# The first Strassen block of two feed-forward parts: load order and the order of VectorE, GpSimd and ScalarE

## The reference

```python
D_MODEL, SEQ, D_FF, FFN_RES, EPS = 1024, 1024, 2816, 0.5, 1e-6

def _rmsnorm(x, g):
    xf = x.astype(jnp.float32)
    y = xf * lax.rsqrt(jnp.mean(xf * xf, axis=-1, keepdims=True) + EPS)
    return (y * g.astype(jnp.float32)).astype(x.dtype)

def _swiglu(h, w_gu, w_down):
    g, u = jnp.split(h @ w_gu, 2, axis=-1)
    return (jax.nn.silu(g) * u) @ w_down

for l in range(DEPTH_2):          # DEPTH_2 = 1
    x = x + FFN_RES * _swiglu(_rmsnorm(x, norm_ffn1[l]), w_ffn1_gu[l], w_ffn1_down[l])
    ...
    x = x + FFN_RES * _swiglu(_rmsnorm(x, norm_ffn2[l]), w_ffn2_gu[l], w_ffn2_down[l])
```

## Time and profile before

| | before |
|---|---|
| runs | 3335.28, 3335.58, 3343.84 us; median 3335.58 |
| the profiled execution | 3338.5 us, with a span of 3336.4 us |
| mean granted clock of TensorE | 0.993 of full speed |
| TensorE busy | 3248.6 us (97% of the span), 19068 matmuls |
| VectorE busy | 1818.1 us (54%), 2813 instructions |
| GpSimd busy | 1803.1 us (54%), 1352 instructions |
| ScalarE busy | 1131.2 us (34%), 2104 instructions |
| first feed-forward part, plain pairs to the third block | about 1179 to 1265 us of the span |
| the same stretch of the second | 1550.87 us later |

### The profile page before, as it was taken

The page is one execution under the profiler, slowest core; times in us unless marked ns, Lnnn a source line. Parts: engine busy times, 40 slices in busy tenths (PEclk is TensorE's granted clock), DMA queues, the critical chain, the costliest instruction groups (busy, mean ns, idle before and its releaser), DMA issues.

```text
span 3336.4 us, 47997 instructions
## 1 busy us (share of the span) xinstructions
PE 3248.6 (97%) x19068; PEld 1655.5 (50%) x19068; DVE 1818.1 (54%) x2813; ACT 1131.2 (34%) x2104; POOL 1803.1 (54%) x1352
## 2 busy tenths in 40 slices
PE   8999998999999799999999999999999999999999
PEld 4555653655565344444445545555545444444444
DVE  4365558236545887775113376665666687676100
ACT  1434422233341523231002455555555342323000
POOL 4555752446675277674333465555665438777332
PEclk9999999999999999999999999999999999999999
DMA  3112112112021211112222111111112121111312
GB/s 133 41 49 62 59 61 90 53 40 77 26 89 39 82 56 58 64 51 98 71 67 93 32 53 53 56 48 52 36 53 90 47 101 53 62 64 38 109 52 79
DMA packets 59275, 211.70 MB, mean 63 GB/s; under 512 B 7344, under 2 KB 7728, under 8 KB 58544
## 3 DMA queue, kind: packets, MB, share of 16 engines
q1 hardware_dynamic: 54304, 191.34, 17.6%
q10 hardware_dynamic: 4752, 17.30, 1.3%
HBM read 181.36 MB, written 20.97 MB: 61 GB/s over the span
## 4 chain that ended last, share of the span: by engine, by line
PE 94%; DVE 3%; issue 1%; ACT 1%; POOL 1%; DMA 0%; DVEq 0%; POOLq 0%; ACTq 0%
PE pair L1184 27%; PE pair L1185 26%; PE pair L1186 26%; PE pair L1404 3%; PE pair L1373 3%; PE pair L1385 2%; PE pair L1622 1%; PE pair L1648 1%; PE pair L1633 1%; PE pair L1576 1%; PE pair L1204 1%; DVE arena L2155 1%; PE pair L1362 0%; POOL panel_parts L967 0%; ACT residual L1905 0%
## 5 line engine op out<-in xcount | busy, mean ns | idle before, releaser
L1184 PE MATMUL pair<-operand,panel_parts 128*128 128x512 f16 x1808 | 693.2, 383 | 47.8 <-DVE operand L2155 26.1
L966 POOL TENSOR_SCALAR panel_parts<-panel_raw 128x1024 f16<-128x1024 f32 (+3 forms) x204 | 209.0, 1024 | 920.7 <-issue 654.4
L1185 PE MATMUL pair<-operand,panel_parts 128*128 128x512 bf16 x1808 | 690.6, 382 | 0.0
L1186 PE MATMUL pair<-operand,panel_parts 128*128 128x512 f16 x1808 | 690.4, 382 | 0.0
L1184 PE MATMUL pair<-arena,panel_parts 128*128 128x512 f16 (+1 forms) x1248 | 471.3, 378 | 8.9 <-issue 4.4
L967 POOL TENSOR_TENSOR panel_parts<-panel_raw,panel_parts 128x1024 bf16<-128x1024 f32 (+3 forms) x204 | 469.2, 2300 | 17.0
L1003 POOL TENSOR_SCALAR arena<-arena,row_inv 128x256 f32<-128x256 f32 (+7 forms) x256 | 344.6, 1358 | 236.4 <-DVE row_inv L2221 236.1
L1185 PE MATMUL pair<-arena,panel_parts 128*128 128x512 bf16 (+1 forms) x1248 | 470.5, 377 | 0.0
L1186 PE MATMUL pair<-arena,panel_parts 128*128 128x512 f16 (+1 forms) x1248 | 470.3, 377 | 0.0
L1184 PEld LDWEIGHTS pair<-operand,panel_parts 128*128 128x128 f16 x1808 | 177.5, 98 | 283.1 <-issue 94.8
L2158 DVE SCALAR_TENSOR_TENSOR residual<-pair,residual 128x1024 f32<-128x1024 f32 (+1 forms) x64 | 61.3, 958 | 420.0 <-PE pair L1186 392.1
(11 more groups left out here) (300 smaller groups left out, 5979.1 us busy)
## 6 DMA issues: line engine op xcount, KB each, us to landing
panel_raw<-in_wl SPq DMA_DIRECT2D x58, 512.0 KB, 3.5
panel_raw<-in_wm SPq DMA_DIRECT2D x56, 512.0 KB, 3.6
ffn_extra<-in_wgu SPq DMA_DIRECT2D x18, 1024.0 KB, 5.0
panel_raw<-in_wgu SPq DMA_DIRECT2D x18, 1024.0 KB, 5.1
panel_raw<-in_wdn SPq DMA_DIRECT2D x32, 512.0 KB, 3.5
residual<-residual_spill SPq DMA_DIRECT2D x31, 512.0 KB, 6.9
residual_spill<-residual ACTq DMA_DIRECT2D x24, 512.0 KB, 2.6
panel_raw<-in_wgu SPq DMA_DIRECT2D x16, 512.0 KB, 3.6
```

Source lines behind the costliest of these rows:

```text
L966: chained(nc.gpsimd.tensor_scalar(hi[:, c], RAW[:, s, c], HI_MAX, -HI_MAX, ALU.min, ALU.max))
L1184: nc.tensor.matmul(out, stat[0], mov[0], start=first, stop=False, skip_group_check=skip)
L1185: nc.tensor.matmul(out, stat[0], mov[1], start=False, stop=False, skip_group_check=skip)
L1186: return nc.tensor.matmul(out, stat[1], mov[0], start=False, stop=last, skip_group_check=skip)
```

## The change

- `SQT`: the eight squares have their homes in 8192 columns of `arena`, none in `EXR`.
- SP: the raw weights of block 0 are loaded right behind the first turn's four panels, with no wait; the other blocks' loads are as they were.
- ScalarE: `weight_part(0, 0)` stands behind the first SiLU instead of the second; `term_part(B_T4)` stands before the weights 5 and 6 instead of behind them.
- GpSimd: `term_rest(B_T4)` stands behind `weight_rest(0, 4)` instead of `weight_rest(0, 6)`.
- VectorE: the four `weight_sum(0, n)` stand before `plain_pair(1)`; `plain_pair(3)` is cut into `plain_front(3)` and `plain_back(3)`, with `term_clip(B_T4)` and `evict(0, 0)` between them; `evict(0, 1)` and `evict(0, 2)` stand before the `weight_sum(1, n)`.

No arithmetic is added or left out. The diff:

```diff
--- before.py
+++ after.py
@@ -464,7 +464,7 @@
         GAINED, SQSUM, ROOT = [SIL[1], AF[1]], STAT[:, 0:T], STAT[:, T:2 * T]
         EX = sb("ffn_extra", [P, 4608])
         EXR = EX[:, 0:2048]
-        SQT = [arena(c, 1024) for c in (11264, 12288, 26624, 27648, 22528, 24576)] + [EXR[:, 0:1024], EXR[:, 1024:2048]]
+        SQT = [arena(8192 + 1024 * k, 1024) for k in range(KT)]
         SILP, AFP = [arena(2048 + 1024 * s, 1024) for s in range(2)], [arena(4096 + 1024 * s, 1024) for s in range(2)]
 
         XPF = XP.rearrange("p a c -> p (a c)")
@@ -865,21 +865,24 @@
                     layer_panel(l, name)
 
             def ffn(idx):
+                def raw(b):
+                    f = PLAIN_F + b
+                    dst = EXR.rearrange("p (j c) -> p j c", j=2) if b % 2 == 0 else RAW[:]
+                    src = io[f"wgu{idx}"][f // 2, 2 * (f % 2):2 * (f % 2) + 2].rearrange("j p c -> p j c")
+                    sp.dma_start(dst, src).then_inc(raw_loaded[b % 2], 16)
+
                 for i in range(PLAIN_F // 2):
                     for j in range(4):
                         panel(f"gu{idx}", i, j, io[f"wgu{idx}"][i, j])
-                for b in range(BLOCKS):
-                    f = PLAIN_F + b
-                    if b == 0:
-                        sp.wait_ge(square_added, 7 * idx)
-                    elif b == 1:
+                    if i == 0:
+                        raw(0)
+                for b in range(1, BLOCKS):
+                    if b == 1:
                         for j in (2, 3):
                             sp.wait_ge(panel_split[panel_slot(f"gu{idx}", j)], panels_before(f"gu{idx}", PLAIN_F // 2 - 1, j) + 2)
                     else:
                         sp.wait_ge(weight_lo, 7 * block_of(idx, b - 1))
-                    dst = EXR.rearrange("p (j c) -> p j c", j=2) if b % 2 == 0 else RAW[:]
-                    src = io[f"wgu{idx}"][f // 2, 2 * (f % 2):2 * (f % 2) + 2].rearrange("j p c -> p j c")
-                    sp.dma_start(dst, src).then_inc(raw_loaded[b % 2], 16)
+                    raw(b)
                 sp.wait_ge(weight_lo, 7 * BLOCKS * idx)
                 for i in range(2):
                     for j in range(12):
@@ -1073,9 +1076,11 @@
                     nc.gpsimd.tensor_tensor(lo, q, hi, ALU.subtract).then_inc(term_ready_pool, 1)
 
                 term_rest(B_T2, Q22, 0)
-                for i in range(7):
+                for i in range(5):
                     weight_rest(0, i)
                 term_rest(B_T4, Q21, 1)
+                for i in range(5, 7):
+                    weight_rest(0, i)
                 for b in range(1, BLOCKS):
                     for i in range(7):
                         weight_rest(b, i)
@@ -1959,17 +1964,18 @@
                     nc.scalar.activation(SILH[h], SILH[h], ACT.Silu).then_inc(half_silu, 1)
 
                 plain_silu(0)
+                weight_part(0, 0)
                 for home, q, n in ((B_T1, Q11, 9), (B_T3, Q12, 10), (B_T2, Q22, 11)):
                     term_part(home, q, n)
                 plain_silu(1)
-                for i in range(5):
+                for i in range(1, 5):
                     weight_part(0, i)
                 for f in range(2, PLAIN_F):
                     plain_silu(f)
+                act.wait_ge(tile_ready[3], tiles_before(f"gu{idx}", PLAIN_F // 2, 3))
+                term_part(B_T4, Q21, 12)
                 for i in range(5, 7):
                     weight_part(0, i)
-                act.wait_ge(tile_ready[3], tiles_before(f"gu{idx}", PLAIN_F // 2, 3))
-                term_part(B_T4, Q21, 12)
                 for b in range(BLOCKS):
                     first_copy(b)
                     if b + 1 < BLOCKS:
@@ -2566,12 +2572,19 @@
                 restart()
 
                 def plain_pair(f):
+                    plain_front(f)
+                    plain_back(f)
+
+                def plain_front(f):
                     i, j = divmod(f, 2)
                     g = ready(f"gu{idx}", i, 2 * j)
                     tt(AFP[j], g[:, :], ROOT, ALU.mult).then_inc(tile_taken[2 * j], 1)
                     u = ready(f"gu{idx}", i, 2 * j + 1)
                     dve.wait_ge(silu_made[j], i + (PLAIN_F // 2 * (idx - 1) + 1))
                     tt(AFP[j], u[:, :], SILP[j], ALU.mult).then_inc(tile_taken[2 * j + 1], 1)
+
+                def plain_back(f):
+                    i, j = divmod(f, 2)
                     dve.wait_ge(tile_taken[2 * j + 1], tiles_before(f"gu{idx}", i, 2 * j + 1) + 1)
                     chained(tt(AFP[j], AFP[j], ROOT, ALU.mult))
                     t = slice(f * T, (f + 1) * T)
@@ -2651,25 +2664,32 @@
                 term_sum(Q12, Q22, Q12, 10, 9)
                 term_sum(Q22, Q22, Q11, 11, 10)
                 term_sum(Q21, Q21, Q22, 12, 11)
-                plain_pair(1)
                 for n in range(4):
                     weight_sum(0, n)
+                plain_pair(1)
                 term_clip(B_T2, 3).then_inc(term_clipped, 1)
                 term_split(B_T1, Q11, 1)
                 plain_pair(2)
                 term_split(B_T3, Q12, 2)
-                plain_pair(3)
+                plain_front(3)
                 term_clip(B_T4, 4).then_inc(term_clipped, 1)
+                evict(0, 0)
+                plain_back(3)
                 for b in range(BLOCKS):
                     more = b + 1 < BLOCKS
                     if b > 0:
                         keep_block(b - 1)
-                    evict(b, 0)
+                    if b > 0:
+                        evict(b, 0)
+                    else:
+                        evict(b, 1)
+                        evict(b, 2)
                     if more:
                         for n in range(4):
                             weight_sum(b + 1, n)
-                    evict(b, 1)
-                    evict(b, 2)
+                    if b > 0:
+                        evict(b, 1)
+                        evict(b, 2)
                     for step in (3, 4, 5):
                         evict(b, step)
                 keep_block(BLOCKS - 1)
```

## The result

| | before | the change |
|---|---|---|
| median of the 19 runs of each | 3339.49 us (3335.28 to 3343.95) | 3345.63 us (3341.73 to 3349.92) |
| ratio, 95% interval | | 1.0015 (1.0009 to 1.0021) |
| the profiled execution, its span | 3338.5, 3336.4 us | 3341.73, 3339.6 us |

The change makes the kernel slower by 0.15% (5.0 us, 3.0 to 7.0, by the ratio; the two medians lie 6.1 us apart). That is less than the 0.3% which a few runs can tell from no change; it took 19 of each.

A forecast was written before the change was run, and what follows sets the result against it. TensorE bounds the kernel, with 13.0 us of its waits and low clock to win. Per feed-forward part 5.81 + 1.11 + 2.54 + 1.7 (clock) = 11.16 us; 22.3 for both, less 13.0, is +9.3 on 3335.6: 3344.9 us, range 3329 to 3350.

The forecast's parts named there:

- (a): VectorE's four weight sums, now before the second plain pair, meet GpSimd's panel split: 5.4 us, 2.8 more, done at 1194.4.
- (b): VectorE's second plain pair runs into the next panel's split, waits for its clip and subtraction, and ends at 1203.8.
- (c): VectorE's remainder waits for GpSimd's 2048-column remainder, issued first: ends at 1211.2 against 1205.03, 6.1 us late.
- (d): Third pair and remainder end at 1223.7; the fourth pair's second half starts at 1226.0 instead of 1219.73.
- (e): ScalarE's copies follow to 1229.2, the eviction ends at 1230.0: first block's fourth product 2.85 us late (0.68 before).
- (f): Pair's second half waits for GpSimd's moved remainder; first block's sixth product 5.81 us late in total, against 4.49.
- (g): Second block's sums lie between third and fourth eviction; the second block's fourth product comes 1.11 us later than possible.
- (h): Third block's sums wait for GpSimd's sixth weight of the second (1253.3); second block's sixth product 2.54 us late.
- rival A: VectorE keeps its place, fourth product on time, sixth 0.5 late, second-block waits stay: -1.4 us, 3334.2; chance 0.14 with D.
- B: The stall goes whole, second-block waits too, GpSimd's sixth weight done by 1246: -12.0 us, 3323.6; chance 0.13.
- C: As forecast, but the lag reaches the third block and each gap costs 2.7 of clock: 3350 us; chance 0.07.
- D: The change does nothing, TensorE's late products being held by GpSimd's weights alone: 3335.6 us; chance 0.14 with A.

The follow-up runs named there:

- Experiment 3: The changed kernel with GpSimd's 2048-column remainder for B_T2 issued as four instructions of 512 columns: ratio 1.0008 to before.
- 1: The changed kernel with the four weight sums of block 0 behind plain_pair(1) again: ratio 0.9993 to before.
- experiment 4: The changed kernel with evict(0, 1) and evict(0, 2) behind the second block's weight sums again: ratio 1.0033 to before.
- 6: The changed kernel with plain_pair(3) in one piece, B_T4's clip and evict(0, 0) behind it: ratio 1.0013 to before.
- 5: The changed kernel with GpSimd's remainder for B_T4 back behind the block's last weight: ratio 1.0020 to before.
- 7: The kernel before with only the squares' new homes and the early raw load of block 0: ratio 1.0006 to before.
- the first of 11: The kernel before with evict(b, 1) and evict(b, 2) ahead of the next block's weight sums in the first two blocks alone: ratio 0.9985.
- 2: The kernel before with the early raw load, its homes and the four weight sums ahead of plain_pair(1): ratio 1.0033 to before.
- 10: The kernel before with evict(0, 1) and evict(0, 2) ahead of the second block's weight sums, in the first block alone: ratio 0.9987.
- 8: The kernel before with evict(b, 1) and evict(b, 2) ahead of the next block's weight sums in every block: ratio 0.9951.
- second of 11: The kernel before with evict(b, 1) and evict(b, 2) ahead of the next block's weight sums from the third block on: ratio 0.9985.

## Why the prediction was right

It said slower, +9.3 us, by VectorE and GpSimd meeting at other places. Measured: 5.0 us (3.0 to 7.0) in the timed runs, 7.3 us in the two parts of the profile. So direction and mechanism held, and the size was put too high: 9.3 lies outside the interval. That the time itself came so near, 3344.9 foreseen and 3345.63 measured, is luck: the median of three runs that it was added to was 3.9 us below that of 19, which makes up for most of the excess.

- **(a), (b)** were right: sums of 1.52 and 2.50 us, all four done at 1190.2, that is 1194.3 in the times of before (1194.4 predicted), and a pair behind which the next instruction starts at 1199.64, that is 1203.7 (1203.8).
- **(c)** was right: a row of 6.04 us where VectorE's remainder was predicted to wait. Experiment 3 shows that it is the length of GpSimd's instruction, and 1 that it hangs on the sums' place.
- **(d), (e)**: the fourth pair's second row at 1225.9 in the times of before (1226.0); product 4 2.69 late (2.85).
- **(f)**: product 6 5.66 late (5.81). "About 4 us worse" without the moved evictions: 5.1 at product 6 itself, but only 2.0 and 3.2 in the lateness of a whole part (experiment 4), since the moved evictions bring waits to the second block. "About 1" for the split pair: 0.2 to 0.5 at product 6, nothing in the whole (6).
- **(g), (h)**: 1.04 (1.11) and 2.52 (2.54). The wait for GpSimd's sixth weight of the second block is there: it ends at 1248.99, that is 1253.1 in the times of before (1253.3). The rival A had these two right as well, and experiment 1 brings A about: product 4 on time, product 6 0.5 late, the second block's two waits as they were. B needed that weight by 1246 and falls. C falls, since the third block has no wait, and D, since the time did change.
- **The clock's 1.7** came in part 1 (1.38 and 0.3 behind the 2.37 us gap) and not in part 2.
- **From 9.3 to 7.3.** Waits and low clock together are 20.7 us in the change (22.3 predicted) and 13.0 before, as predicted: 7.7. What is missing is the clock's 1.7 in part 2 and 0.25 a part in the waits, less 0.56 for the wait in the fourth block of part 2, which the prediction does not have.
- **What the sum lacked** is in the line "the rest of the blocks run without a wait". Slots are lost there, 3.3 us in one part of before and 2.8 in one part of the change. They nearly cancel in these two profiles, which is luck again: 16.3 us instead of 13.0 were there to win, and the change has 23.5 (10.9 + 9.8 + 2.8) against them, 7.3 more before rounding.
- **From 7.3 to 5.0** is open. One profile is one execution, and slots and low clock move a part by several us from one to the next.

The Trainium skill's rule (SBUF — State Buffer, "Who interferes with whom"), that the first to ask holds the shared port pair for its whole instruction, is what experiment 3 shows: 6.04 us beside one instruction of 2048 columns, 3.13 beside the first of four pieces.

## What to carry to other kernels

When two engines take turns, an instruction costs what it meets, so a move is to be replayed against the other engine's list and not only against its own. Put what TensorE waits for (evictions) ahead of what is merely next (sums for the next block), in every round of the loop and not only in the first, since the delay otherwise moves on by a block: here that order alone is worth 0.5%, where the change with its five parts cost 0.15%. And measure a stage whole, from a first to a last event: the loss of 0.2 us in every round stood in no list of waits.

## What was not expected of the hardware

- **A wait of one matmul hides inside TensorE's records.** Neighbours 0.44 us apart, each 0.38 long, show no idle time; 15 of them are 3.3 us.
- **The slots are lost, or not, for a whole part.** Parts 1 and 2 of before run the same lists and differ by 0.2 us at product 4 of the first block; 3.3 us of slots are lost in the one, none in the other. Of the other profiles with the old order in the later blocks, 1, 5, 7 and the first of 11 lost them in both parts, 2, 6 and the change in one, 3, 4 and 10 in none. The new order takes the wait away: the eviction then ends 0.54 us early in nearly every later block (8, and second of 11). Which rhythm a part falls into goes with the low clock. Where the last wait of over half a microsecond was the one at product 6 of the second block, the six parts with 1.6 to 1.7 us of low clock behind it lost no slots, and the six with none behind it lost them. In the kernel before, 1.5 us of low clock in the first block went with slots (part 1) and 2.7 with none (part 2). A later TensorE gives GpSimd time to get ahead; that this is the cause was not tested. It makes a difference of 3.3 us in either part from one execution to the next, so single profiles of such kernels are compared term by term.
- **The low clock behind a gap is not certain.** After a gap of 2.37 us ahead of the same product, TensorE's matmuls came 0.43 us apart, the lower of its two levels, for 1.7 us of loss in part 1 of the change, for 1.7 in both parts of 3, for 1.6 and 1.7 in 10, and not at all in part 2 of the change, in 1 and in part 2 of 5. Nor is it a matter of length alone: gaps of 2.75 us ahead of product 6 of the first block (3) cost none, and one of 2.51 (part 1 of 5) cost none where the same gap cost 1.7 in part 2.
